# Two-layer network in float32 on one core: the products' operands start at other bytes of their partitions

## What is computed

```
def swiglu(h, w1, w3, w2):
    return (jax.nn.silu(h @ w1) * (h @ w3)) @ w2

    # first block
    merged = g[:, :, 0] * p_a + g[:, :, 1] * p_b + g[:, :, 2] * p_c
    x = x + gate_m * (merged @ w_out[l])
    u = causal_dwconv(h @ w_up[l], ffn_conv_w[l], ffn_conv_b[l])
    u_gate, u_val = jnp.split(u, 2, axis=-1)
    x = x + gate_f * ((jax.nn.silu(u_gate) * u_val) @ w_down[l])
    # second network: layer 0 dense, layer 1 the experts
    f = swiglu(tokens, ff_w1[k], ff_w3[k], ff_w2[k])
    f = moe_swiglu(tokens, moe_router[k], moe_w1[k], moe_w3[k], moe_w2[k])
```

## Time and profile before

| | us |
|---|---|
| median of 3 runs | 2055.96 |
| lowest and highest | 2055.66 to 2056.51 |
| span of the profiled execution | 2055.1 |
| TensorE busy in it | 2009.1 |
| VectorE busy | 1703.8 |
| ScalarE busy | 1256.9 |

### The profile page before, as it was taken

The page is one execution under the profiler, slowest core; times in us unless marked ns, Lnnn a source line. Parts: engine busy times, 40 slices in busy tenths (PEclk is TensorE's granted clock), DMA queues, the critical chain, the costliest instruction groups (busy, mean ns, idle before and its releaser), DMA issues.

```text
span 2055.1 us, 32745 instructions
## 1 busy us (share of the span) xinstructions
PE 2009.1 (98%) x13665; PEld 1791.2 (87%) x13665; DVE 1703.8 (83%) x1874; ACT 1256.9 (61%) x1269; POOL 39.5 (2%) x77
## 2 busy tenths in 40 slices
PE   7999999999899999999999999999999999999997
PEld 6899999999879899999878888888888888888886
DVE  6787988988786768887479898898888988898987
ACT  3468745654434454443367777777777777777775
POOL 3010000000000000000000000000000000000000
PEclk8999999999999999999999999999999999999999
DMA  9874776768643459999259999999999999999994
GB/s 310 290 249 137 244 248 198 261 224 292 207 161 123 138 170 332 316 316 323 84 204 369 369 342 373 344 372 355 356 358 352 365 352 367 357 348 372 361 370 157
DMA packets 337576, 589.16 MB, mean 287 GB/s; under 512 B 10517, under 2 KB 150315, under 8 KB 337424
## 3 DMA queue, kind: packets, MB, share of 16 engines
q1 hardware_dynamic: 333776, 580.70, 80.7%
q0 software_dynamic: 3008, 5.78, 1.1%
q10 hardware_dynamic: 640, 0.52, 0.1%
HBM read 585.89 MB, written 1.07 MB: 286 GB/s over the span
## 4 chain that ended last, share of the span: by engine, by line
PE 89%; DVE 5%; ACT 2%; issue 2%; DMA 1%; SPq 0%; DVEq 0%; ACTq 0%
PE bk L657 15%; PE bk L659 15%; PE bk L658 15%; PE bk L651 11%; PE bk L653 11%; PE bk L652 11%; DVE wlo L1957 1%; DVE macc L1982 1%; PE bk L1202 1%; ACT whi L1339 1%; DMA raw<-in_w_mod 1%; PE bk L1251 1%; PE bk L713 1%; PE bk L1114 1%; PE bk L715 1%
## 5 line engine op out<-in xcount | busy, mean ns | idle before, releaser
L1957 DVE TENSOR_TENSOR wlo<-raw,whi 128x2048 fp32r<-128x2048 f32 x477 | 1080.9, 2268 | 223.1 <-ACT whi L1339 222.2
L1339 ACT CAST whi<-raw 128x2048 fp32r<-128x2048 f32 x477 | 903.2, 1894 | 389.5 <-PE bk L659 259.0
L651 PE MATMUL bk<-HH,whi 128*128 128x256 f32 x1480 | 425.1, 287 | 0.7 <-DVE KC L2233 0.4
L652 PE MATMUL bk<-HL,whi 128*128 128x256 f32 x1480 | 417.5, 282 | 0.0
L653 PE MATMUL bk<-HH,wlo 128*128 128x256 f32 x1480 | 417.2, 282 | 0.0
L657 PE MATMUL bk<-whi,xh 128*128 128x512 f32 x896 | 354.6, 396 | 0.0
L659 PE MATMUL bk<-wlo,xh 128*128 128x512 f32 x896 | 349.4, 390 | 0.0
L658 PE MATMUL bk<-whi,xl 128*128 128x512 f32 x896 | 348.7, 389 | 0.0
L651 PEld LDWEIGHTS bk<-HH,whi 128*128 128x128 f32 x1480 | 282.4, 191 | 6.4 <-issue 3.8
L652 PEld LDWEIGHTS bk<-HL,whi 128*128 128x128 f32 x1480 | 282.5, 191 | 1.1 <-issue 0.7
L653 PEld LDWEIGHTS bk<-HH,wlo 128*128 128x128 f32 x1480 | 282.4, 191 | 0.0
(11 more groups left out here) (378 smaller groups left out, 2471.5 us busy)
## 6 DMA issues: line engine op xcount, KB each, us to landing
raw<-in_moe_w SPq DMA_DIRECT2D x334, 1024.0 KB, 6.1
raw<-in_ada_w SPq DMA_DIRECT2D x56, 1024.0 KB, 5.5
raw<-in_ff_w SPq DMA_DIRECT2D x40, 1024.0 KB, 5.8
raw<-in_w_in SPq DMA_DIRECT2D x29, 1024.0 KB, 5.4
raw<-in_w_mod SPq DMA_DIRECT2D x24, 1024.0 KB, 5.8
raw<-in_w_up SPq DMA_DIRECT2D x22, 1024.0 KB, 5.2
raw<-in_attn_w_qkv SPq DMA_DIRECT2D x12, 1024.0 KB, 5.5
raw<-in_w_branch SPq DMA_DIRECT2D x8, 1024.0 KB, 4.9
```

The lines of the kernel that those rows point to most:

```text
L651: pe.matmul(o, sh, mh, start=start, stop=False, skip_group_check=True)
L652: pe.matmul(o, sh, ml, start=False, stop=False, skip_group_check=True)
L1339: act.copy(whi[k][:, :n], raw[q.slot[i]][:, :n]).then_inc(q.hi_done.mark(g), 1)
L1957: dve.tensor_tensor(wlo[k][:, :n], raw[q.slot[i]][:, :n], whi[k][:, :n].bitcast(F), ALU.subtract).then_inc(q.taken.mark(i), 1)
```

## The change

Three things are moved, all of them addresses; instructions, their order, their shapes, waits and transfers are the same on every engine.

1. `sb` takes a place (`skew`) for a tensor. HH and HL get 64, OH 32, OL 0, HHc and HLc 4 (one word off), HH2, HL2, FH, FL 32, HH4 32, HL4 96, FH4 and FL4 96, HH5 and HL5 0, xh and xl 32, tth and ttl 0. What lies behind them moves along (YH, YL from 96 to 0, pb and ptt from 0 to 32; TH and TL stay at 96).
2. The six slab buffers get 64 bytes more each, so that they lie at 0, 64, 0 (`whi`) and 64, 0, 64 (`wlo`) in place of 0 throughout. Within each number modulo 3 the pair differs by 64.
3. `halves_at` shifts a slab's data inside its buffers by 8 or 16 words, by tag: both halves 32 bytes for "w1", "w2", "dn", "ug", "f1", only `wlo` 32 for "uv", only `whi` 32 for "f3", both 64 for "f2", none for "w3" and the rest.

What moves against what is stationary, in places, before and after ("32/96" is 32 or 96 by the buffer's number):

| stage | moving | stationary |
|---|---|---|
| mixer, output | HH, HL 0 -> 64 | slabs 0 -> 0/64 |
| branches | OH 0 -> 32, OL 0 -> 0 | slabs 0 -> 0/64 |
| ug, dn | HH2, FH and lows 0 -> 32 | slabs 0 -> 32/96 |
| uv | HH2, HL2 0 -> 32 | whi 0 -> 0/64, wlo 0 -> 32/96 |
| q and k of the attention | HH2, HL2 0 -> 32 | slabs 0 -> 0/64 |
| context, wo | HHc, HLc 0 -> 4 | slabs 0 -> 0/64 |
| f1 | HH4 32 -> 32, HL4 32 -> 96 | slabs 0 -> 32/96 |
| f3 | as f1 | whi 0 -> 32/96, wlo 0 -> 0/64 |
| f2 | FH4, FL4 32 -> 96 | slabs 0 -> 0/64 |
| fn | HH5, HL5 32 -> 0 | slabs 0 -> 0/64 |
| w1 | slabs 0 -> 32/96 | xh, xl 0 -> 32 |
| w3 | slabs 0 -> 0/64 | xh, xl 0 -> 32 |
| w2 | slabs 0 -> 32/96 | tth, ttl 96 -> 0 |

```diff
-        def sb(name, shape, dt=F):
-            t = nc.alloc_sbuf_tensor_at(name, shape, dt, offset=at[0])
+        def sb(name, shape, dt=F, skew=None):
+            if skew is None:
+                t = nc.alloc_sbuf_tensor_at(name, shape, dt, offset=at[0])
+            else:
+                at[0] = (at[0] + 127 - (skew & ~31) & ~127) + (skew & ~31)
+                e = skew % 32 // 4
+                t = nc.alloc_sbuf_tensor_at(name, [shape[0], e + n // 4], dt, offset=at[0])[:, e:e + n // 4]
+                n += 4 * e
+                if len(shape) == 3:
+                    t = t.rearrange("p (a b) -> p a b", a=shape[1])
-        whi = [sb(f"whi{i}", [128, 2048], R) for i in range(NP)]
-        wlo = [sb(f"wlo{i}", [128, 2048], R) for i in range(NP)]
+        whi = [sb(f"whi{i}", [128, 2064], R) for i in range(NP)]
+        wlo = [sb(f"wlo{i}", [128, 2064], R) for i in range(NP)]
...
-        HH, HL = sb("HH", [128, 8, S], R), sb("HL", [128, 8, S], R)
+        HH, HL = sb("HH", [128, 8, S], R, 64), sb("HL", [128, 8, S], R, 64)
...
-        OH, OL = sb("OH", [128, 16, S], R), sb("OL", [128, 16, S], R)
+        OH, OL = sb("OH", [128, 16, S], R, 32), sb("OL", [128, 16, S], R, 0)
-        HHc, HLc = sb("HHc", [128, 8, S], R), sb("HLc", [128, 8, S], R)
-        HH2, HL2 = sb("HH2", [128, 8, S], R), sb("HL2", [128, 8, S], R)
+        HHc, HLc = sb("HHc", [128, 8, S], R, 4), sb("HLc", [128, 8, S], R, 4)
+        HH2, HL2 = sb("HH2", [128, 8, S], R, 32), sb("HL2", [128, 8, S], R, 32)
-        FH, FL = sb("FH", [128, 22, S], R), sb("FL", [128, 22, S], R)
+        FH, FL = sb("FH", [128, 22, S], R, 32), sb("FL", [128, 22, S], R, 32)
...
-        HH4, HL4 = sb("HH4", [128, 8, S], R), sb("HL4", [128, 8, S], R)
-        FH4, FL4 = sb("FH4", [128, 28, S], R), sb("FL4", [128, 28, S], R)
+        HH4, HL4 = sb("HH4", [128, 8, S], R, 32), sb("HL4", [128, 8, S], R, 96)
+        FH4, FL4 = sb("FH4", [128, 28, S], R, 96), sb("FL4", [128, 28, S], R, 96)
-        HH5, HL5 = sb("HH5", [128, 8, S], R), sb("HL5", [128, 8, S], R)
+        HH5, HL5 = sb("HH5", [128, 8, S], R, 0), sb("HL5", [128, 8, S], R, 0)
...
-        XH = [sb(f"xh{i}", [128, 8, 256], R) for i in range(2)]
-        XL = [sb(f"xl{i}", [128, 8, 256], R) for i in range(2)]
+        XH = [sb(f"xh{i}", [128, 8, 256], R, 32) for i in range(2)]
+        XL = [sb(f"xl{i}", [128, 8, 256], R, 32) for i in range(2)]
-        TT = [sb(f"tth{i}", [128, 4, 128], R) for i in range(2)]
-        TTL = [sb(f"ttl{i}", [128, 4, 128], R) for i in range(2)]
+        TT = [sb(f"tth{i}", [128, 4, 128], R, 0) for i in range(2)]
+        TTL = [sb(f"ttl{i}", [128, 4, 128], R, 0) for i in range(2)]
...
+        lies = {"w1": (8, 8), "w3": (0, 0), "w2": (8, 8), "dn": (8, 8), "ug": (8, 8), "uv": (0, 8), "f1": (8, 8), "f3": (8, 0), "f2": (16, 16)}
+        def halves_at(q, g):
+            i = q.gi[g]
+            e, n, k = lies.get(q.plan[i][1][0], (0, 0)), q.plan[i][3] * q.plan[i][4], g % NP
+            return whi[k][:, e[0]:e[0] + n], wlo[k][:, e[1]:e[1] + n]
-            k, nk, w = q.pg % NP, q.plan[i][3], q.plan[i][4]
+            nk, both = q.plan[i][3], halves_at(q, q.pg)
-            return [v[:, :nk * w].rearrange("p (k n) -> p k n", k=nk) for v in (whi[k], wlo[k])] + [nk]
+            return [v.rearrange("p (k n) -> p k n", k=nk) for v in both] + [nk]
...
-            n, k = q.plan[i][3] * q.plan[i][4], g % NP
+            n = q.plan[i][3] * q.plan[i][4]
-            act.copy(whi[k][:, :n], raw[q.slot[i]][:, :n]).then_inc(q.hi_done.mark(g), 1)
+            act.copy(halves_at(q, g)[0], raw[q.slot[i]][:, :n]).then_inc(q.hi_done.mark(g), 1)
...
-            i, k = q.gi[g], g % NP
-            n = q.plan[i][3] * q.plan[i][4]
+            i = q.gi[g]
+            n, (high, low) = q.plan[i][3] * q.plan[i][4], halves_at(q, g)
-            dve.tensor_tensor(wlo[k][:, :n], raw[q.slot[i]][:, :n], whi[k][:, :n].bitcast(F), ALU.subtract).then_inc(q.taken.mark(i), 1)
+            dve.tensor_tensor(low, raw[q.slot[i]][:, :n], high.bitcast(F), ALU.subtract).then_inc(q.taken.mark(i), 1)
```

## The result

The changed kernel takes 2059.86 us (median of 10 runs, 2058.9 to 2061.83) against 2055.93 for the one before (10 runs, 2055.07 to 2057.39). The ratio is 1.0019, with a 95% interval of 1.0011 to 1.0027. The forecast was 2031.7 us, 24.3 us faster; measured is 3.9 us slower. The span of the profiled execution went from 2055.1 to 2059.7 us.

The account below looks back on a forecast made before the run. The prediction took the distance between TensorE's matmul starts to bound the kernel. Two prices for operand places, applied stage by stage, summed to -24.3 us, from 2055.96 to 2031.7 us, with a range of 1980 to 2060.

Parts of the forecast that it names:

- the weak spot: Places taken as the cause of differing start distances, though no stage in the trace differed only in a place.
- moving at 32 in place of 0, -3.3 ns: Price per matmul, 116.7 - 120 ns, from f1 and f3 against the up part, applied wherever moving operands go to 32 or 96.
- stationary at 0 in place of 96, -6.5 ns: Price per matmul, 227.1 - 233.6 ns, from w1 and w3 against w2, applied to w2.
- w2, -13.2: Experts' w2: 1344 matmuls gain both prices, 6.5 + 3.3 ns each, -13.2 us; the largest term.
- w1, -4.4: Experts' w1: 1344 matmuls gain 3.3 ns each from the moving operand's place, -4.4 us.
- w3, 0: Experts' w3: its slabs move at 0/64, so no gain or loss by the moving operand's price.
- rival B: Only the two places' difference modulo 64 counts; w3 pays +8.7 us, sum +9.7, 2065.7 us, slower; chance 0.15.
- HHc, 0, with bounds -1.3 and +2.7: HHc and HLc one word off, 384 matmuls: no row had such a place; between -1.3 and +2.7 us, taken as 0.
- D: Rival: places do nothing, stages differ by what surrounds them; 2056 us; chance 0.13.
- C: Rival: moving and stationary reads collide when placed alike; apart, much excess goes; 1996 to 1958 us; chance 0.22 in some size.
- E: Rival: TensorE gets faster but the experts' weights don't come faster; only other stages' -6.7 us left, 2049 us; chance 0.10.
- the cover argument: VectorE wrote 128x512 in 685 ns at places 32 and 0, so slab rounding at other places was costed at nothing.

Follow-up runs that it names:

- x2_act32: Kernel before with only the moving operands of the 256-column stages at place 32, slabs at 0; 2047.85 us against 2056.8, ratio 0.9957.
- x3_xh32: Kernel before with xh and xl alone moved from place 0 to 32, tth and ttl held at 96; 2069.78 us against 2056.8, ratio 1.0063.
- z1_alike: Kernel before with slabs, xh, xl, tth, ttl alike, 32 bytes further on; moving operands of 256-column stages left at 128 modulo 256; 2043.97 us, ratio 0.9942.
- y1_tt: Survey on the kernel before: xh, tth and the moving operands of 256-column stages at various starts modulo 512 from the slabs'; 2049.74 us, single run.
- x4_pads: Kernel before with the slab buffers alone 64 bytes longer, no data shifted in them; 2053.95 us against 2056.8, ratio 0.9987.
- y4_both: Kernel before with slabs, xh, xl, tth, ttl alike modulo 256 and moving operands of 256-column stages 32 bytes behind; 2036.74 us, ratio 0.9906.
- y2_map: Second survey on the kernel before, with other starts modulo 512 for xh, tth and the moving operands of 256-column stages; 2063.28 us, single run.

## Why the prediction was wrong

**The bound** was read rightly: TensorE's starts set the time, and the change of 3.9 us in the distances appears as 4.6 in the span. That places move the distance, taken as the weak spot, holds (x2_act32, x3_xh32).

**The step that failed** is the one that turned two differences between stages into prices of one operand's own place: "moving at 32 in place of 0, -3.3 ns" and "stationary at 0 in place of 96, -6.5 ns". In the 512-column stages what counts is whether the two operands start alike modulo 256 (z1_alike, y1_tt); in the 256-column ones it is their difference with its sign, and not even that alone. From this step came two terms that the prediction put at nothing: xh and xl going from 0 to 32, the stationary operand of w1 and w3, got no price (alone it cost 13 us, x3_xh32), and neither did the slab buffers going to 0 and 64 (alone it cost the experts 5.6 us of distances, x4_pads). And two prices were carried over to forms where no row had them: the first, read at 256 columns, to w1 and w2 with 512, and the second, read from +96 to +0, to a tth that came to lie elsewhere. The places were taken modulo 128, and so two things could not be seen: how far apart modulo 256 the slab buffers at 0 and 64 come to lie, and that place 0 for tth is not the slabs' place. Term by term, forecast against measured sums:

- w2, -13.2: measured -1.4 us. It moved from one layout out of step to another; in step it gains 9.6 (y4_both), still less than forecast.
- w1, -4.4: measured +1.9 us (228.0 to 229.6 ns). The shift kept its places equal to xh's modulo 64, and equal modulo 128 in part, but the padding parts the halves.
- w3, 0: measured +7.5 us (226.8 to 232.7). This is the largest measured term, and the one that rival B priced at +8.7.
- HH2 (up, q and k), -4.8: -2.5 us. dn, -1.7: -0.9 us. Branches, -0.8: -0.6 us. The sign is right and the price half: 118 in place of 117.
- f1, f3 and f2, 0: +2.1 us. They were at +32 before, 117.2, and went to mixed differences (118.5 and 117.7).
- fn, +0.6: +0.2 us.
- Mixer and output, 0: -2.5 us, and `natural` -0.8. I took 64 as 0 is taken; it is not.
- HHc, 0, with bounds -1.3 and +2.7: +1.0 us.

**The rivals.** B came nearest in the mechanism: its sign, its w3, and that the 512- and 256-column forms go opposite ways, which I had held against it. Its modulus (64) was wrong, as x4_pads shows, and so its +9.7 missed the gain of the mixer and of `natural` (3.3 us) and put f1 and f3 too high. (It also left out HHc, which by its own rule gains 384 x 3.3 = 1.3 us.) D's 2056 is nearer to the measured time, by luck: gains of 4.0 us and a loss of 8.0 largely cancel. C's remark that a smaller distance may be found by another pattern is half true: OH and OL at +64 stand at 115.0, but no layout came near the 109 of columns + 2.6. D falls with x2_act32, E with y4_both, where the experts get 9.8 us shorter (972.7 for 982.5 us) and the weights keep up, in slices of up to 376 GB/s. Of the cover argument, 685 ns for VectorE at two places, nothing needs to be taken back: its 128x2048 subtraction has a mean of 2290 ns in both kernels, 465 times.

**The rule of the skill.** The Trainium skill, "SBUF — State Buffer", section "Who interferes with whom", gives TensorE two independent read ports, one for the moving operand and one for the weight load, and says that it never waits on anyone. No run here shows TensorE held up by another engine's reads. But the place of the stationary operand alone lengthened the distances of w1 and w3 by 5.3 and 6.4 ns (x3_xh32), so two independent ports are not the whole account of how the two reads go together, and the measurement decides; which part of the chip joins them no run shows.

**What stays open.** Why the step has 32 clocks and the period 256 bytes: 120.0 and 226.7 ns are 256 and 512 columns and 32 clocks at 2.4 GHz, and a step that long would fit reads that take turns in a fixed round, but that is argued, not shown. Why fn falls into step at +128 and the branches don't, and why +64 stands at 115.0 in the branches and at 117.8 in dn, no run tells: the difference is the same. No run changes what the other engines read and write at the same time.

## What to carry to other kernels

Where matmuls follow each other without a gap, measure the distance between starts against columns / 2.4 GHz and look whether stages of one shape differ by their operands' addresses. In this kernel the 512-column fp32r products wanted stationary and moving operands, both halves alike, at one start modulo 256 (227 in place of 233 ns), and the 256-column ones wanted the moving operand 32 or 64 bytes behind the stationary one (115 to 118 in place of 120) and not one word (123). Padding between buffers of a ring is a change of layout too, and a place read modulo a guess can hide what matters: vary one operand at a time before pricing it.

## What the runs showed of the hardware beyond that

- With all operands alike modulo 256, nearly every distance is the same to 1 ns (90 to 98% of them are 120 in the mixer, up and dn stages of the kernel before; 97% of them 226 or 227 in w3 of y4_both), once the step is reached: right behind the transposes, before w1, it takes seven to ten matmuls. Other differences can be as steady: fn has nothing but 116 and 117 at +32 (y4_both) and nothing but 120 at +128 (y2_map). Most run through patterns, for example 235, 231, 235, 232, 235, 232 ns in x3_xh32.
- Being in step is the better state with 512 columns (13.4 ns over the columns against 16 to 21). With 256 it is at 13.3, where +32 and +64 have 8 to 11, +96 has 13.3 as a mean, and one word off has 16.6.
- The expert stages drew 350 GB/s on average in the kernel before and slices of up to 376 GB/s in y4_both.
